# Prompt attention: reciprocals and last products of a strip three steps later, maxima transposed and copied one step later

## What is computed

```
s = jnp.einsum('bqhd,bkhd->bhqk', qi, k).astype(jnp.float32) * ATTN_SCALE
mask = k_chunk[None, :] <= qc[:, None]
s = jnp.where(mask[None, None], s, NEG)
p = jax.nn.softmax(s, axis=-1).astype(v.dtype)
return jnp.einsum('bhqk,bkhd->bqhd', p, v)
```

## Time and profile before

| what | value |
|---|---|
| median of three runs | 3293.43 us (3290.76 to 3295.22) |
| the profiled execution | 3279.37 us |
| its span | 3277.6 us |
| granted TensorE clock, mean | 0.944 |
| PE busy | 2999.3 us (92% of the span) |
| DVE, ACT, POOL busy | 1592.0, 1363.0, 1381.3 us |
| prompt attention, from 437 to 1004 us | 567 us, 17% of the span |

### The profile page before, as it was taken

The page is one execution under the profiler, slowest core; times in us unless marked ns, Lnnn a source line. Parts: engine busy times, 40 slices in busy tenths (PEclk is TensorE's granted clock), DMA queues, the critical chain, the costliest instruction groups (busy, mean ns, idle before and its releaser), DMA issues. The chain is left out here.

```text
span 3277.6 us, 44278 instructions
## 1 busy us (share of the span) xinstructions
PE 2999.3 (92%) x15336; PEld 2618.4 (80%) x15336; DVE 1592.0 (49%) x2176; ACT 1363.0 (42%) x2635; POOL 1381.3 (42%) x824
## 2 busy tenths in 40 slices
PE   6996979999995849999969999999999999999997
PEld 5775757777774747888869999998999999899996
DVE  3543777767761324443334444346444445544446
ACT  4233447767773322222133433344334334444443
POOL 5242236655653232222224334356343346544444
PEclk9997979999996569999989999999999999999999
DMA  4225531122203142222242122133221222422221
GB/s 125 73 74 89 174 101 38 40 57 42 43 17 91 46 168 91 83 87 82 66 172 77 51 64 77 51 93 138 64 77 51 64 77 78 142 77 77 77 77 57
DMA packets 165334, 264.44 MB, mean 81 GB/s; under 512 B 48784, under 2 KB 91952, under 8 KB 164048
## 3 DMA queue, kind: packets, MB, share of 16 engines
q1 hardware_dynamic: 165232, 263.15, 27.0%
HBM read 206.83 MB, written 56.27 MB: 80 GB/s over the span
## 5 line engine op out<-in xcount | busy, mean ns | idle before, releaser
L2013 POOL TENSOR_TENSOR ff_w_lo<-ff_w_raw,ff_w_hi 128x1024 fp32r<-128x1024 f32 x198 | 519.5, 2650 | 751.3 <-ACT ff_w_hi L2085 751.3
L84 PE MATMUL ff_u<-ff_x_hi,ff_w_hi 128*128 128x384 f32 (+1 forms) x2112 | 691.3, 327 | 32.5 <-POOL ff_w_lo L2013 20.5
L86 PE MATMUL ff_u<-ff_x_lo,ff_w_hi 128*128 128x384 f32 (+1 forms) x2112 | 690.7, 327 | 0.0
L85 PE MATMUL ff_u<-ff_x_hi,ff_w_lo 128*128 128x384 f32 (+1 forms) x2112 | 690.6, 327 | 0.0
L84 PEld LDWEIGHTS ff_u<-ff_x_hi,ff_w_hi 128*128 128x128 f32 x2112 | 400.0, 189 | 34.8 <-POOL ff_w_lo L2013 21.0
L85 PEld LDWEIGHTS ff_u<-ff_x_hi,ff_w_lo 128*128 128x128 f32 x2112 | 399.8, 189 | 1.1
L86 PEld LDWEIGHTS ff_u<-ff_x_lo,ff_w_hi 128*128 128x128 f32 x2112 | 399.7, 189 | 0.0
L2207 DVE SCALAR_TENSOR_TENSOR ff_cv_a<-ff_up_a,ff_taps,ff_cv_a 128x768 f32<-128x768 f32 (+1 forms) x132 | 157.7, 1194 | 369.7 <-ACT ff_cv_a L2134 361.7
L2228 DVE TENSOR_TENSOR ff_y<-ff_y,ff_d 128x512 f32<-128x512 f32 x374 | 239.6, 681 | 146.3 <-PE ff_d L86 146.2
L84 PE MATMUL ff_d<-ff_w_hi,ff_h_hi 128*128 128x512 f32 x748 | 291.3, 389 | 4.4 <-DVE ff_y L2228 4.4
L85 PE MATMUL ff_d<-ff_w_hi,ff_h_lo 128*128 128x512 f32 x748 | 291.5, 390 | 0.0
(11 more groups left out here) (356 smaller groups left out, 6267.8 us busy)
## 6 DMA issues: line engine op xcount, KB each, us to landing
ff_w_raw<-in_w_ffn_p SPq DMA_DIRECT2D x198, 512.0 KB, 3.6
pj_raw<-in_x_t SPq DMA_DIRECT2D x40, 256.0 KB, 3.0
mx_work<-in_w_mix_p SPq DMA_DIRECT2D x18, 512.0 KB, 4.1
mx_m_raw<-scratch_mix_t SPq DMA_DIRECT2D x17, 512.0 KB, 5.2
mx_x_raw<-in_x SPq DMA_DIRECT2D x17, 512.0 KB, 4.0
scratch_x_t<-mx_work SPq DMA_DIRECT2D x17, 512.0 KB, 3.2
scratch_y<-mx_work SPq DMA_DIRECT2D x17, 512.0 KB, 2.9
ff_y<-scratch_y SPq DMA_DIRECT2D x17, 512.0 KB, 7.2
```

Of the source, the lines that this page charges most:

```text
L84: pe.matmul(out, lh, rh, start=first, stop=False, **kw)
L85: pe.matmul(out, ll, rh, start=False, stop=False, **kw)
L86: return pe.matmul(out, lh, rl, start=False, stop=last, **kw)
L2013: pool.tensor_tensor(w_lo[:, slot], w_raw[:, n % RAWS, :].rearrange("p (k c) -> p k c", c=P), f32(w_hi[:, slot]), ALU.subtract).then_inc(w ...
```

## The change

Three of four constants change. No instruction is added or taken away.

```diff
-ROW_AFTER, COPY_AFTER, REC_AFTER, NORM_AFTER = 3, 1, 6, 11
+ROW_AFTER, COPY_AFTER, REC_AFTER, NORM_AFTER = 4, 1, 9, 14
```

## The result

The changed kernel takes **3273.85 us** (median of 6 runs, 3269.96 to 3279.7) where the kernel before takes 3292.71 (6 runs, 3285.58 to 3295.22): ratio 0.9947, 95% interval 0.9935 to 0.9959. That is 0.53% faster.

A forecast was written before the change was run, and what follows sets the result against it. PE bounds the prompt attention, leaving its idle time and slow clock to win. Gains of 4.1, 4.2, 0.4 and 0.5 us less 1.0 for start and 1.0 for loads net 7.2, from 3293.4 to about 3286.5 us; range 3276 to 3302.

The forecast's parts named there:

- ScalarE's new wait: Step 16 of heads 1 to 7: the copy waits for the moved last product, 3.0 us, 7 times.
- Reciprocal: Three steps later, VectorE's wait for sums from DRAM falls from 2.03 us to 0 to 0.4; PE's 0.89 us go.
- Head 0: Stall at the turn for head 1's first strip goes, 2.4 us, with its slow clock, 1.7: 4.1 us won.
- Heads 1 to 6: Stall moves from the turn to step 24's peak, behind a delayed low part; 0.7 us a head won, 4.2 us.
- In the others some 2 us of the stall are left, so I count none back: Slow clock behind turns outside head 0: no time regained, with a bound of 5.1 us.
- Loads: Key loads behind a head's third-strip reciprocals move three steps later: 0.2 us a head, 1 us lost; bounds 0 and 9.
- Start: The second strip's turn and row copy move just ahead of its first scores: 1.0 us lost, 0 to 2.
- the prediction's own list: Signs of error: scores waiting for exponentials or row copies, long low parts, key waits over 1 us, PE idle unchanged.
- Head 7 and end: Head 7 without a split wins 0.9 less 0.5 for the late peak, 0.4; the end wins 0.5 us.
- The first: Rival: VectorE is also locked out behind the product after the values' split; 3294 us, no change, chance 0.22.
- The second: Rival: ACT's stand at step 16's copy becomes PE's, up to 2.2 us 7 times; 3300 us, chance 0.18.
- The fourth: Rival: VectorE gets the port at each GpSimd operation's end, so turn stalls and slow clock go; 3272 us, chance 0.07.

The follow-up runs named there:

- second pair: Profiled executions of unedited repeats of the kernel before and the changed kernel; medians 3290.67 and 3273.6 us, ratio 0.9947.
- before again: The kernel before repeated with no edit, for its spread and another trace; 3290.67 us, ratio 1.0008.
- first pair: The original profiled executions of the kernel before and the changed kernel, 3279.37 and 3269.96 us.
- the later split on the change: The changed kernel with GpSimd's split of the next head's values one step later; 3290.46 us, ratio 0.9990 to the kernel before.

## Why the prediction was wrong, and where it was right

- **ScalarE's new wait.** Forecast about 3.0 us, 7 times; measured 3.13 six times and 2.70. Right, and so was the late peak behind it (0.5 us forecast, 0.51 measured).
- **Reciprocal.** Wait in step 17 under 0.5 us: none in heads 1 to 6, 0.76 us in head 7. Right but for the last head.
- **Head 0.** Turn stall gone and clock back: 4.1 us forecast. From unit 16 of head 0 to head 1's first scores the change takes 4.2 us less, in both pairs. Right.
- **Heads 1 to 6.** Mechanism right, sizes off. The split began 12.66 us behind the scores of unit 16 where my hand timing gave 13.1, the low part got in at its end, and the peak stalled 1.67 us where I had some 2: 1.0 us a head instead of 0.7, 1.8 us in all.
- **The step that failed most: "In the others some 2 us of the stall are left, so I count none back."** The clock gave 2.5 us in one pair and 6.1 in the other. The bound of 5.1 us lies between them; zero as the value was not. The falls cost 1.5 us a head where they cost 1.7 to 3, in five of twelve heads where it was six. That a shorter stall causes this is not shown: the reciprocal alone has turn stalls of 1.8 us and falls in five heads of six. In the five traces without a fall in heads 1 to 6 no stall there was over 1.24 us. The medians point the same way, by the estimate of some 10 us of clock under the result. The prediction had set aside that the profiled execution lay 14 us below the median, because "the change is in stalls that both have"; the stalls repeat, the falls behind them do not.
- **Loads.** 1.0 us charged; ScalarE waited for keys twice, 1.6 us at the start of the phase (the kernel before does so too in its second trace, 1.5 us) and 0.3 us later, and the distance to before is 4.11 us at head 1's first scores and 4.13 at those of unit 8: nothing reached TensorE.
- **Start.** 1.0 us charged. The later row copy keeps the first scores of the second strip waiting 0.84 us, 0.68 in the second pair, where before again waited 0.30: the mechanism is right. By the prediction's own list, scores that wait for a row copy were a sign of being wrong, though it had priced this one. The net at head 1 is another matter: 4.1 us won where 4.1 less 1.0 was forecast, and 3.7 in the second pair. Traces differ by more than that ahead of unit 16 (first scores between 451.4 and 455.5 us, then 40.1 to 43.7 us for 16 units), so this 1.0 us in the sum is luck.
- **Head 7 and end.** 0.9 us won by forecast; 0.5 won in the first pair and 0.3 lost in the second.
- **The sum.** First pair: 7.2 + 1.8 (heads 1 to 6) + 2.5 (clock) + 1.0 (loads) + 1.0 (start) - 0.4 (head 7, end) = 13.1, as measured. Second: 7.2 + 1.8 + 6.1 + 1.0 + 0.6 - 1.2 = 15.5. I had taken the charges near their middle and the gain of the clock at its least. The 3 to 6 us by which the medians' 18.9 exceed these sums no trace itemises. (7.2 taken from 3293.4 is 3286.2, not the 3286.5 written.)
- **Rivals.** The first (lock-out behind the product) is what the product's move does alone, 3.61 us. The second is half true: no exponential ever kept TensorE waiting, but the stand costs 2.8 us a head all the same (64.2 against 61.4 with a third slot), through the low parts of VectorE and GpSimd. I wrote it off as covered, because I looked only at who waits for ScalarE directly. The fourth's time (3272) is 2 us from the result by luck: the low part still took 2.43 us, the peak still stalled, and the clock still fell in two heads.
- **What was not asked.** I costed the turn's move at "0.7 us a head" with the rest of the change in place, and took 0.7 for its price. Alone it brings 1.6 us a head and no clock fall in heads 1 to 6 (63.3 to 63.9 us each). It moves a copy on ScalarE too, and VectorE asks later by it; but the copy alone left the low part passed over, so which part does how much is not shown. Nor did I look at the 0.67 us stall of step 12, which is there before and after.

## What to carry to other kernels

When a stall traces back to an operation that took five times its usual time, name what held it and move that: one step for one GpSimd operation was worth more than the three numbers of the change. A reorder that adds a wait for a buffer is to be costed with one more slot for that buffer; here 0.7% hung on it. Parts of such a change do not add, so time them apart before all are taken.

## What was not expected of the hardware

- VectorE's low part and a GpSimd operation did not run side by side: a low part of 512 columns that asked while one was running was in no trace done less than 0.54 us after that one's end. Which goes next was decided by something else than who asked first. Asked for 0.11 us before the split: 3.81 us, twice passed over the earlier trace rows. Asked 0.29 and 0.37 us behind its start: in at its end (2.44, 2.43 us). Asked 0.35 and 0.63 us behind its start: passed over (3.61, 3.05). In head 2 of the changed kernel the same 0.35 us got in (2.44), so this distance does not decide it. With the later split on the change it asked 0.37 us behind a product's start and was passed over at two ends (4.56, three operations in all). So my reading in the prediction, that one who asks shortly after an operation's start gets in at its end, does not hold. The Trainium skill, page "SBUF — State Buffer", section "Who interferes with whom", says that whoever issues first gets the shared pair for the whole instruction and that the other fully blocks. The block is borne out, but it did not end with the first operation: the one held out may be passed over at further ends. What decides it is left open; in one kernel heads with the same distance come out alike.
- The clock's falls behind a stall do not repeat from one execution to the next (two heads or four, in the same kernel) while the stalls do, and stalls of 1.8 us had more of them (five and six of six heads) than stalls of 2.3: a single trace does not price them.
